# Zero-padded full-array products in a gated recurrence and a forgetting attention, and a state product placed one tile later

## What is computed

```
b = cumsum(logf) within a chunk;  b_mid, b_last = b at the middle and at the end
A = (q*exp(b-b_mid)) @ (k*exp(b_mid-b)).T, lower triangle only;   o_intra = A @ v
dS = (k*exp(b_last-b)).T @ v;   S_next = exp(b_last)*S + dS
o = o_intra + (q*exp(b)) @ S_prev
```

```
logits = einsum(q, k) * scale + F[:, :, s0:s1, None] - F[:, :, None, :s1]
p = softmax(where(mask, logits, -1e30));   o = einsum(p, v)
```

## Time and profile before

| | |
|---|---|
| time, median of 3 runs | 3085.66 us (3085.48 to 3087.09) |
| span of the profiled execution, first to last instruction | 3083.3 us |
| TensorE matmul, busy | 3026.1 us, 98% |
| VectorE / ScalarE / GpSimd, busy | 61% / 53% / 22% |
| share of the chain that ended last | PE 92%, DVE 5%, ACT 2% |
| HBM traffic | 164 GB/s over the span |

### The profile page before, as it was taken

The page is one execution under the profiler, slowest core; times in us unless marked ns, Lnnn a source line. Parts: engine busy times, 40 slices in busy tenths (PEclk is TensorE's granted clock), DMA queues, the critical chain, the costliest instruction groups (busy, mean ns, idle before and its releaser), DMA issues.

```text
span 3083.3 us, 63457 instructions
## 1 busy us (share of the span) xinstructions
PE 3026.1 (98%) x25252; PEld 2947.4 (96%) x25252; DVE 1885.8 (61%) x3274; ACT 1629.6 (53%) x2604; POOL 667.0 (22%) x292
## 2 busy tenths in 40 slices
PE   8999999999999999989999999999999999999999
PEld 7999998999999998869999989999999999999999
DVE  5555556744544558767777788654457865554554
ACT  5766766566678743565444443444444444444443
POOL 3333333444444333214444400000000000000000
PEclk9999999999999999999999999999999999999999
DMA  5444443454444454415555544555554455555554
GB/s 192 148 139 147 141 145 123 168 175 164 164 139 145 139 184 150 137 55 191 178 179 185 182 138 139 187 185 187 189 190 165 152 180 190 189 181 188 190 190 163
DMA packets 72288, 506.67 MB, mean 164 GB/s; under 512 B 7904, under 2 KB 10464, under 8 KB 11232
## 3 DMA queue, kind: packets, MB, share of 16 engines
q1 hardware_dynamic: 71584, 503.16, 47.8%
q10 hardware_dynamic: 576, 1.72, 0.2%
HBM read 502.75 MB, written 2.10 MB: 164 GB/s over the span
## 4 chain that ended last, share of the span: by engine, by line
PE 92%; DVE 5%; ACT 2%; issue 1%; DMA 0%; SPq 0%; DVEq 0%; ACTq 0%
PE bank L451 12%; PE bank L452 12%; PE bank L453 12%; PE bank L465 5%; PE bank L2285 4%; PE banks L2285 4%; PE bank L2286 4%; PE banks L2286 4%; PE bank L2287 4%; PE banks L2287 4%; PE banks L2061 3%; PE banks L2062 3%; PE banks L2063 3%; PE bank L2061 2%; PE bank L2062 2%; PE bank L2063 2%
## 5 line engine op out<-in xcount | busy, mean ns | idle before, releaser
L428 ACT ACTIVATE whi<-raw 128x1024 fp32r<-128x1024 f32 x898 | 941.1, 1057 | 970.2 <-PE bank L453 391.4
L435 DVE TENSOR_TENSOR wlo<-raw,whi 128x1024 fp32r<-128x1024 f32 x667 | 820.1, 1241 | 446.5 <-ACT whi L428 445.3
L435 POOL TENSOR_TENSOR wlo<-raw,whi 128x1024 fp32r<-128x1024 f32 x231 | 610.1, 2642 | 965.1 <-ACT whi L428 965.0
L451 PE MATMUL bank<-xa_hi,whi 128*128 128x272 f32 (+1 forms) x2000 | 582.3, 291 | 7.0 <-DVE wlo L435 5.7
L452 PE MATMUL bank<-xa_lo,whi 128*128 128x272 f32 (+1 forms) x2000 | 572.2, 286 | 0.0
L453 PE MATMUL bank<-xa_hi,wlo 128*128 128x272 f32 (+1 forms) x2000 | 571.1, 286 | 0.0
L451 PEld LDWEIGHTS bank<-xa_hi,whi 128*128 128x128 f32 x2000 | 375.8, 188 | 12.6 <-issue 7.5
L452 PEld LDWEIGHTS bank<-xa_lo,whi 128*128 128x128 f32 x2000 | 377.1, 189 | 1.3
L453 PEld LDWEIGHTS bank<-xa_hi,wlo 128*128 128x128 f32 x2000 | 376.0, 188 | 0.0
L451 PE MATMUL bank<-xb_hi,whi 128*128 128x256 f32 (+1 forms) x1120 | 318.4, 284 | 1.5 <-DVE wlo L435 1.5
L452 PE MATMUL bank<-xb_lo,whi 128*128 128x256 f32 (+1 forms) x1120 | 316.3, 282 | 0.0
(11 more groups left out here) (443 smaller groups left out, 6732.6 us busy)
## 6 DMA issues: line engine op xcount, KB each, us to landing
raw<-in_w SPq DMA_DIRECT2D x251, 1024.0 KB, 4.8
raw<-in_v SPq DMA_DIRECT2D x128, 1024.0 KB, 5.2
raw<-in_u SPq DMA_DIRECT2D x96, 1024.0 KB, 4.8
hT<-in_hT SPq DMA_DIRECT2D x4, 544.0 KB, 8.2
out<-hT SPq DMA_DIRECT2D x8, 256.0 KB, 2.3
r_keys<-in_keys ACTq DMA_DIRECT2D x1, 1024.0 KB, 4.7
c_mask<-in_masks ACTq DMA_DIRECT2D x1, 320.0 KB, 2.7
g_mask<-in_masks SPq DMA_DIRECT2D x1, 272.0 KB, 12.2
```

Of the source, the lines that this page charges most:

```text
L428: act.activation(whi[:, (2 * t.q + half) % 4, :], raw[:, t.q, half * 1024:(half + 1) * 1024], ACT.Copy).then_inc(w_hi_done, 1)
L435: eng.tensor_tensor(wlo[:, t.q, at], raw[:, t.q, at], whi[:, slot, :].bitcast(F32), ALU.subtract).then_inc(w_lo_done[half], 1)
L451: te.matmul(ps, hi, x[0][:, kk, cols], start=(kk == 0), stop=False)
```

## The change

The three small row heights go: `g.v`, `g.kst`, `g.att` and `f.pm` are cleared once at the start, so that rows which no copy writes are zero, and the products read all 128 rows. Chunks 1 and 2 become one product with 256 moving columns, of the keys of token block 0 and a new tensor `g.vpair` that holds v of rows 0 to 63 in its first 128 columns and v of rows 64 to 127 in its second, zero elsewhere. The dS products go first in the group, then the products into `B_O`; the semaphore between them is dropped. L708 uses 128 weight columns. The state product moves from behind t[3] to behind the next step's t[0]; the square on ScalarE moves behind the rounding of t[2]'s weights; `qe` moves on VectorE behind the evacuation of t[1] and the low part of t[3]'s weights and leaves `factors_done`. ScalarE makes two more copies a head. `f.pm` takes 128 partitions and GpSimd clears it once.

```diff
+            g.vpair = tensor(st, "g_vpair", [P, 2, P])
-                f.pm = tensor(s2, "f_pm", [META, 3, P])
+                f.pm = tensor(s2, "f_pm", [P, 3, P])
@@ hgrn_tensor, body
                     project(te, t[0], xa, cols_all)
+                if within(h - 2, HEADS):
+                    te.wait_ge(states_done, h - 1)
+                    for c_ in range(1, NCH + 1):
+                        cs = slice(META + CH * (c_ - 1), META + CH * c_)
+                        last = te.matmul(B_O[:, cs], g.state[:, c_ - 1, :], g.qe[:, cs], start=False,
+                                         stop=(c_ == NCH))
+                    last.then_inc(o_done, 1)
...
-                    te.matmul(B_AT[0:META, 2 * P:MASK_H], g.ki[:, 0:META], g.qi[:, 0:META], start=True, stop=True)\
+                    te.matmul(B_AT[:, 2 * P:MASK_H], g.ki[:, 0:P], g.qi[:, 0:META], start=True, stop=True)\
...
-                    for c_ in (0, 1, 3, 2):
-                        cs, rows, n = span(c_)
-                        if c_ == 2:
-                            te.matmul(B_O[:, 0:META], g.v[0:META, 2, :], g.att[0:META, 2 * P:MASK_H], start=True,
-                                      stop=False).then_inc(lower_rows, 1)
-                            for m, cols in enumerate(tok):
-                                te.matmul(B_O[:, cols], g.v[:, m, :], g.att[:, m * P:(m + 1) * P], start=False,
-                                          stop=False)
-                            te.wait_ge(lower_rows, h)
-                        ds = te.matmul(B_DS[:, c_ * P:(c_ + 1) * P], g.kst[rows, n, :], g.v[rows, n, :],
-                                       start=True, stop=True)
-                    ds.then_inc(ds_done, 1)
+                    te.matmul(B_DS[:, 0:P], g.kst[:, 2, :], g.v[:, 2, :], start=True, stop=True)
+                    te.matmul(B_DS[:, P:3 * P], g.kst[:, 0, :], g.vpair[:], start=True, stop=True)
+                    te.matmul(B_DS[:, 3 * P:4 * P], g.kst[:, 1, :], g.v[:, 1, :], start=True, stop=True)\
+                        .then_inc(ds_done, 1)
+                    te.matmul(B_O[:, 0:META], g.v[:, 2, :], g.att[:, 2 * P:MASK_H], start=True, stop=False)
+                    for m, cols in enumerate(tok):
+                        te.matmul(B_O[:, cols], g.v[:, m, :], g.att[:, m * P:(m + 1) * P], start=False, stop=False)
...
-                if within(p, HEADS):
-                    te.wait_ge(states_done, h)
-                    for c_ in range(1, NCH + 1):
-                        cs, _, _ = span(c_)
-                        last = te.matmul(B_O[:, cs], g.state[:, c_ - 1, :], g.qe[:, cs], start=False,
-                                         stop=(c_ == NCH))
-                    last.then_inc(o_done, 1)
@@ hgrn_scalar, body
+                if within(h, HEADS):
+                    split_hi(act, t[1].next())
                 if within(h - 2, HEADS):
                     act.wait_ge(o_done, h - 1)
                     act.activation(g.osq[:], B_O[:, 0:L], ACT.Square).then_inc(osq_done, 1)
-                if within(h, HEADS):
-                    split_hi(act, t[1].next())
...
+                    act.activation(g.vpair[0:CH, 0, :], B_VT[0:CH, 0:P], ACT.Copy)
+                    act.activation(g.vpair[CH:P, 1, :], B_VT[CH:P, 0:P], ACT.Copy)
@@ hgrn_vector
-            ve.memset(g.att[:], 0.0).then_inc(preset, 1)
+            for t in (g.att, g.v, g.kst, g.vpair):
+                last = ve.memset(t[:], 0.0)
+            last.then_inc(preset, 1)
...
-                    ve.tensor_tensor(g.qi[:], g.qs[:], g.e_mid[:], ALU.mult)
-                    ve.tensor_tensor(g.qe[:], g.qs[:], g.e_cum[:], ALU.mult).then_inc(factors_done, 1)
+                    ve.tensor_tensor(g.qi[:], g.qs[:], g.e_mid[:], ALU.mult).then_inc(factors_done, 1)
                 if within(h, HEADS):
                     evac(t[1], g.fr)
                     split_lo(ve, t[2].next(), 0)
+                if within(p, HEADS):
+                    need(ve, o_done, p)
+                    ve.tensor_tensor(g.qe[:], g.qs[:], g.e_cum[:], ALU.mult)
@@ qz_scalar
+                        if static(h) and h == 2:
+                            act.wait_ge(pm_set, 1)
-                        act.activation(f.pm[:], B_PM[0:META, 0:3 * P].rearrange("p (a b) -> p a b", a=3), ACT.Copy)
+                        act.activation(f.pm[0:META, :, :],
+                                       B_PM[0:META, 0:3 * P].rearrange("p (a b) -> p a b", a=3), ACT.Copy)
@@ qz_pool
                         po.wait_ge(kn_done, HEADS)
+                        po.memset(f.pm[:], 0.0).then_inc(pm_set, 1)
```

More of the change, by code:

```diff
@@ L637, in build @@
         ds_done = sem("ds_done")
-        lower_rows = sem("lower_rows")
         states_done = sem("states_done")
@@ L648, in build @@
         tok = [slice(META, META + P), slice(META + P, L)]
[L650 to L655, removed]
         IN_ALL = 16 * 2
@@ L1077, in build @@
         sums_turned = sem("sums_turned")
+        pm_set = sem("pm_set")
         def qz_tensor(te, ch):
```

## The result

The changed kernel takes 3061.11 us (median of 4 runs, 3059.79 to 3061.99), the kernel before 3085.57 beside it (3082.94 to 3087.09). The ratio is 0.992, with a 95% interval of 0.9907 to 0.9932: 24.5 us faster. By the interval the gain lies between 21 and 29 us. The profiled execution spans 3060.2 us, 23.1 less than before.

The account below looks back on a forecast made before the run. TensorE's own matmul stream was taken as the bound, with no engine making it wait. Savings of 17.1 + 1.7 + 5.9 = 24.7 us take the median from 3085.7 to 3061.0 us, range 3056.5 to 3066.5.

Parts of the forecast that it names:

- Chunk group: Recurrence products between t[2] and t[3] on TensorE: 2.62 to 1.55 us, saving 1.07 a head, 17.1 us for 16 heads.
- L708: Meta tokens' attention product on 128 weight columns: saves 0.11 us a head, between 0 and 0.2, 1.7 us for 15 heads.
- Attention: L1093 on 128 rows in the attention's output: saves 0.39 us a head, 5.9 us for 15 heads.
- The state product on TensorE: Moving its eight instructions one tile later in TensorE's queue changes nothing on TensorE.
- The last heads: Last head's factors stay 1.9 us late, as extra copies and one factor less cancel; next-to-last attention head's gain is lost.
- The room grows to 0.7 to 1.1 us: In each recurrence step, VectorE's factors are done that long before TensorE's key transposes ask, against 0.4 us before.
- Padding that removes nothing: First rival: the 0.18 us belongs to something else, only two instructions a head go, 3.5 us: 3082; chance 0.04.
- The rule of the Trainium skill: Weight loads overlap running matmuls only where row groups differ, so full-height products aren't dense and padding removes nothing or adds.
- The new wait: Rival: ScalarE's queue 1.3 us later, TensorE waits 0.5 us at the key transposes in 15 steps: 3068; chance 0.08.
- The slower case: Rival: t[2]'s low part caught behind GpSimd, then ks; factors 3.9 us late, 45 us lost: 3106; chance 0.03.
- qe later: On VectorE qe meets GpSimd's instruction and takes about 2.5 us; costs nothing, or up to 2.2 us a head without cover.
- the clears: Three more on VectorE at the start, one on GpSimd before the attention: once, nothing or at most 1 us.

Follow-up runs that it names:

- the run with 16 columns: The changed kernel with L708, the meta tokens' attention product, back on 16 weight columns: 3061.24 us, ratio 0.992.
- the added copies: The changed kernel with extra ScalarE scratch copies in front of the exponentials: 3061.76 us with two, 3079.71 us with four chained.
- row groups: The changed kernel with chunks 1 and 2 side by side on rows 0 to 63 and 64 to 127, without the vpair copies: 3063.93 us, ratio 0.9926.
- copies behind the exponentials: The changed kernel with ScalarE's four copies of v behind the four exponentials instead of in front: 3061.15 us, ratio 0.9917.

## Why the prediction was right

**The sum.** Forecast were 17.1 + 1.7 + 5.9 = 24.7 us and 3061.0; measured 24.5 and 3061.11. The terms, by the stream:

- Chunk group: 2.62 to 1.55 us, 1.07 a head, as worked out. Both prices in doubt came out plain: L726 with 256 columns took 0.43 us for its two, and the 16-column product 0.22 in all, though by the row of L729 alone one would say 0.14.
- L708: 0.11 a head, shown both ways by the run with 16 columns. The size was right; why those 16 columns cost it is open. Attention: 5.99 us for the stage, 5.9 forecast.
- The state product on TensorE: forecast 0, measured 0.05 us less a head, 0.7 us in all. One of the two passages between projection and small products is gone, and I hadn't counted those.
- The last heads: forecast unchanged. The factors' wait rose from 1.9 to 2.1 us, and the wait for qn from 0.2 to 0.6, the latter as described.

At 493.43 before the last head's keys, 15 x (1.07 + 0.11) + 0.7 = 18.4 us should be saved and 18.55 were. With the last chunk group 1.07 and the attention 5.99 that makes 25.6. The span shows 23.1. Of the missing 2.5 us, 2.0 are in the stage at the end of the recurrence, which should have given 1.07 and gave -0.94: 0.2 for the last head's wait, and a further stretch at half clock, 483.8 to 487.2, which can cost half of its 3.4 us, 1.7. The other 0.5 are in the unchanged rest. The median came out at 24.5, between the two. That 3061.0 was hit to 0.1 us is luck: the mechanism and the terms were right to a few tenths, but with the same work the stretches at half clock move a span by 2 us, as the run with 16 columns shows, and the kernel before alone moved its median by 3.5 us between sets.

**The unit was mis-sized, the total wasn't.** I divided 1.06 us by six changes and got 0.18. The runs have 0.20 for a change around 128-column products (0.41 for two) and 0.29 for the pair around the 16-column product; five at 0.19 and one at 0.11 make the 1.06. The sixth is cheap because the 16-column product in front of it delays the second start behind it anyway, by 0.08 us. Because the change removes all six, the mean was good enough for it. For the run that changed only the order, and lost the cheap one, it wasn't: 0.10 instead of 0.18 us. The step that failed there is reading the average as the price of each.

**The move.** "The room grows to 0.7 to 1.1 us" was 0.75 by the trace and 0.65 by the added copies. "Cost: nothing" was right. The two added copies were taken too cheap, at 0.3 to 0.5 us, where each delays what follows by 0.28, 0.56 together; without them (row groups, or copies behind the exponentials) the factors are 1.3 us early. With this the room came out at the lower end. Copies and move were costed together, which gave the right sum, but not apart, and so the prediction doesn't say what the move is for: the padded kernel without it waits some 0.2 us in every head, and it is worth 0.29 us a head there, 4 us of the 24.5.

**The rivals.** Padding that removes nothing fell with the starts 0.11 us apart, and once more with the run that put one product back on 16 rows. The rule of the Trainium skill beside it (TensorE: Matmul & The Clock Gate, on packing small matmuls) does not hold on these rows: products on the same 128 rows are dense, their weight loads among running matmuls. The new wait is not there; its place was right, since without the move it is exactly there. The slower case came nearer than its 0.03 says: the first half of its mechanism, the low part of t[2]'s weights caught behind GpSimd, does happen, 3.43 us instead of 1.22. My argument against it, that GpSimd would be over when the exponentials are done, came true (308.97 against 310.46), but it says nothing about an instruction that starts earlier. GpSimd's instruction moved, since ScalarE's rounding, on which it waits, starts earlier. Only the second half failed: VectorE came out 0.45 us before the exponentials. That it did is a margin that I had not worked out: I had checked the phase of the factors and not that of the instruction ahead of them.

**qe later** took 2.63 us for the 2.5 forecast, with VectorE still idle behind it, and the clears show nowhere.

## What to carry to other kernels

In a dense stream of small products count the changes of active rows, not the rows: each costs some 0.2 us here, as much as a whole product of 128 columns, so zero rows that spare the change were the cheaper way here. By these prices two pairs of half-height products side by side would about break even (0.22 us saved a pair against 0.4 for going in and out), an estimate that no run tests. Price a small product up to the second start behind it: the row of a 16-column product shows 0.14 us and it costs 0.22. When a change adds work to one engine and moves work on another, cost the two together and then apart: a move that is worth nothing alone may be what pays for the addition. For every VectorE instruction with two tensors from SBUF, check its new phase against GpSimd's, and that of the instruction ahead of the critical one too.

## What the hardware showed that I had not expected

- A change of rows is paid at two places, 0.10 us ahead of the first instruction on the new rows and 0.10 ahead of the second, and both are visible as distances between starts. Only behind a 16-column product is the second part 0.02.
- Two fp32 products on rows 0 to 63 and 64 to 127, into different banks, start 0.01 us apart.
- TensorE was granted half clock for 27.3 to 47.8 us of the span in these kernels, with nearly the same work in most of them, and a kernel whose recurrence is 1.7 us dearer ended 2.0 us earlier. The executions of the kernel before lie between 3082.9 and 3090.1 us. So the span of one execution can't judge an edit of a few us here; the distances between starts in its own group can, to 0.01 us.
- A VectorE instruction with two tensors from SBUF that starts just behind GpSimd's seems to wait out all of it: GpSimd's ended at 308.97 by the profile, VectorE's 1.08 us later, about the 1.22 that it takes by itself.
